# Routing of a mixture-of-experts layer: the last token tile's normed rows by ScalarE and GpSimd, and half a projection product ahead of the counts

## What is computed

```python
n2 = rms_norm(h, g_ffn[i]).reshape(b * s, d)
h = h + hier_moe(n2, w_group[i], b_group[i], w_router[i], b_router[i], w1[i], w3[i], w2[i]).reshape(b, s, d)
gate = jax.nn.sigmoid(rms_norm(h, g_ple[i]) @ w_ple_gate[i] + b_ple_gate[i])
h = h + gate * (p[i] @ w_ple_proj[i])

def hier_moe(xn, ...):                   # top 2 of 8 experts within the best of 4 groups
    gl = xn @ w_group + b_group
    grp = argmax(gl)
    el = (xn @ w_router + b_router), the 8 columns of grp
    top_l, top_i = lax.top_k(el, 2)
    counts = jnp.bincount(eid, length=32)
    # each expert's tokens are gathered into rows; per block of rows xb of expert e:
    hdn = jax.nn.silu(xb @ w1[e]) * (xb @ w3[e])
    ys = hdn @ w2[e]                     # weighted and added back to its tokens
```

## Time and profile before

| | us |
|---|---|
| median of 3 runs | 1689.8 |
| lowest and highest | 1689.41, 1690.76 |
| the profiled execution | 1689.12 |
| its span, first to last instruction | 1687.2 |

### The profile page before, as it was taken

One profiled execution on the slowest core, in us unless ns is written; L12 is line 12 of the kernel. 1 busy time (PEld: TensorE's weight loads), 2 busy tenths in 40 slices (PEclk: granted clock), 3 DMA queues, 4 the chain that ended last, 5 costly groups with the idle time before them and its releaser, 6 DMA issues.

```text
span 1687.2 us, 20190 instructions
## 1 busy us (share of the span) xinstructions
PE 1666.5 (99%) x7754; PEld 1007.6 (60%) x7754; DVE 882.4 (52%) x1509; ACT 386.7 (23%) x702; POOL 211.1 (13%) x279
## 2 busy tenths in 40 slices
PE   9999999999999999999999999999999999999999
PEld 5877888885433343434334455688855544667664
DVE  3755746765433232323225446666756654677663
ACT  3122212002100000000002212321245524544530
POOL 2334310001100000000001000010234420000000
PEclk9999999999999999999999999999999999999999
DMA  7312113254899999999996123114120021212101
GB/s 282 125 63 113 50 61 124 100 202 185 321 424 426 427 427 425 428 427 427 427 426 243 50 75 125 50 63 164 63 101 1 1 76 56 94 51 77 74 1 50
DMA packets 27715, 308.14 MB, mean 183 GB/s; under 512 B 4383, under 2 KB 4671, under 8 KB 10080
## 3 DMA queue, kind: packets, MB, share of 16 engines
q1 hardware_dynamic: 21168, 288.70, 42.1%
q0 software_dynamic: 6448, 18.10, 3.0%
HBM read 306.06 MB, written 4.19 MB: 184 GB/s over the span
## 4 chain that ended last, share of the span: by engine, by line
PE 92%; DVE 4%; DMA 2%; ACT 1%; issue 1%; POOL 0%; DVEq 0%; SPq 0%; ACTq 0%
PE ps L440 88%; PE ps L443 5%; DMA wring<-in_w 2%; DVE arena L1266 2%; ACT arena L2504 1%; DVE arena L1293 0%; DVE arena L1277 0%; DVE small L1281 0%; POOL small L2944 0%; ACT HT L2504 0%; DVE arena L1271 0%; DVE wring L1266 0%; DVE H L1266 0%; DVE arena L1350 0%; DVE ps L1266 0%
## 5 line engine op out<-in xcount | busy, mean ns | idle before, releaser
L440 PE MATMUL ps<-arena 128*64 128x512 f32 (+13 forms) x2484 | 533.8, 395 | 5.6 <-DMA wring<-in_w 1.7
L440 PEld LDWEIGHTS ps<-arena 128*64 128x64 f32 (+4 forms) x2484 | 249.1, 156 | 224.3 <-issue 213.0
L440 PE MATMUL ps<-wring,arena 128*64 128x512 f32 (+2 forms) x1048 | 345.1, 564 | 0.0
L1266 DVE TENSOR_TENSOR arena<-ps,arena 128x512 f32<-128x512 f32 (+1 forms) x196 | 134.1, 684 | 383.4 <-PE ps L440 230.5
L440 PE MATMUL ps<-wring,HT 128*128 128x512 f32 (+1 forms) x880 | 311.0, 505 | 4.8 <-ACT HT L2504 3.3
L440 PEld LDWEIGHTS ps<-wring,HT 128*128 128x128 f32 x880 | 163.5, 190 | 125.5 <-issue 112.7
L440 PE MATMUL ps<-HT,wring 128*128 128x512 f32 (+2 forms) x656 | 222.1, 501 | 0.0
L2504 ACT ACTIVATE arena<-ps 128x512 f32<-128x512 f32 (+4 forms) x155 | 82.7, 533 | 595.3 <-PE ps L443 305.5
L440 PE MATMUL ps<-wring 128*128 128x256 f32 x864 | 195.7, 380 | 0.0
L440 PEld LDWEIGHTS ps<-wring,arena 128*64 128x64 f32 (+1 forms) x1048 | 131.3, 151 | 87.4 <-issue 82.6
L1266 DVE TENSOR_TENSOR H<-ps,H 128x512 f32<-128x512 f32 x182 | 125.9, 691 | 97.6 <-PE ps L440 96.0
(11 more groups left out here) (125 smaller groups left out, 1007.8 us busy)
## 6 DMA issues: line engine op xcount, KB each, us to landing
wring<-in_w SPq DMA_DIRECT2D x48, 2048.0 KB, 22.8
wring<-in_dense SPq DMA_DIRECT2D x38, 2048.0 KB, 8.2
arena<-in_w SPq DMA_DIRECT2D x36, 2048.0 KB, 21.4
HT<-in_w SPq DMA_DIRECT2D x12, 2048.0 KB, 19.5
arena<-in_rows POOLq DMA_DIRECT2D x29, 256.0 KB, 4.0
wring<-in_dense SPq DMA_DIRECT2D x2, 1024.0 KB, 5.6
H<-in_x SPq DMA_DIRECT2D x4, 512.0 KB, 6.8
arena<-in_relb POOLq DMA_DIRECT2D x8, 256.0 KB, 8.6
```

What stands on the lines that cost most here:

```text
L440: return nc.tensor.matmul(o, l, r, start=start, stop=stop, skip_group_check=True)
L1266: done(nc.vector.tensor_tensor(o, a, b, op), tell)
```

## The change

The last tile's normed rows are no longer VectorE's. ScalarE writes `H[:, 3, :]` times the reciprocal root into `nbB[3]` (one instruction of 128x1024, with the columns reordered) right after its last copy of transposed rows. GpSimd waits for it and multiplies each half by its half of the gain row in place (two instructions of 128x512, signal `last_rows`), waits for them, and stores the rows. TensorE waits for `last_rows` instead of `nb` ahead of a = 3. The readers of the gain rows are now these two GpSimd instructions, so that slot 7's first load waits for them. The first half (k = 0) of `projection(0, 1)` stands ahead of `count`, with its wait for its weights, and the second half where the whole product was.

```diff
@@ TensorE, end of stage_a and stage_b
                 pe.wait_ge(S("wpp0"), 16)
                 for i in range(3):
                     projection(i, 0)
+                pe.wait_ge(S("wpp1"), 16)
+                projection(0, 1, (0,))
...
                 ins.then_inc(f.full, 1)
-                pe.wait_ge(S("wpp1"), 16)
-                projection(0, 1)
+                projection(0, 1, (1,))
...
                 for a in range(4):
-                    pe.wait_ge(S("nb"), saw("nb"))
+                    if a < 3:
+                        pe.wait_ge(S("nb"), saw("nb"))
+                    else:
+                        pe.wait_ge(S("last_rows"), 2)
@@ VectorE, normed_rows and stage_b
                     stt(o, x, small[:, 4 + i:5 + i], w, MUL, MUL, "nb" if h else "v")
-                    if i == 3:
-                        row_done(g[h])
...
                     stt(first[:, a, :], iota[:, 0:128], p8[:, 4 + a:5 + a], first[:, a, :], ALU.is_equal, ADD, "first")
-                normed_rows(3, g_ffn)
+                for h in range(2):
+                    rowed[g_ffn[h][0]] = S("last_rows"), h + 1
                 heard("gx")
@@ ScalarE, end of stage_a
                     for j in ((), (0,), (1, 2), (3,))[i]:
                         turned("B", j)
+                a.wait_ge(S("inv"), 10)
+                act(nbB[3].rearrange("t (k p) -> t k p", k=8), H[:, 3, :].rearrange("t (p k) -> t k p", k=8), ACT.Identity, "rt",
+                    scale=small[:, 7:8])
                 for i in range(3):
                     projected(i, 0)
@@ GpSimd
                 norm_root(i)
-                g.wait_ge(S("nb"), 5 + i)
+                if i < 3:
+                    g.wait_ge(S("nb"), 5 + i)
+                else:
+                    g.wait_ge(S("rt"), saw("rt"))
+                    for h, r in enumerate(ROWSEQ_B[2:]):
+                        o = nbB[3].rearrange("t (k p) -> t k p", k=8)[:, :, 64 * h:64 * h + 64]
+                        nc.gpsimd.tensor_tensor(o, o, rowbuf[r % NR].rearrange("t (p k) -> t k p", k=8), MUL
+                                                ).then_inc(S("last_rows"), 1)
+                    g.wait_ge(S("last_rows"), 2)
                 g.dma_start(n2d[i * 128:i * 128 + 128, :], nbB[i]).then_inc(S(f"keep{i % 2}"), 16)
```

## The result

| | before | after |
|---|---|---|
| median of 18 runs, us | 1690.27 | 1692.68 |
| lowest and highest | 1689.21, 1691.32 | 1690.60, 1694.61 |
| profiled execution, its span | 1689.12, 1687.2 | 1692.38, 1690.5 |

The ratio after to before is 1.0015 (95% interval 1.0008 to 1.0021): the change makes the kernel slower by 2.5 us, and the forecast was 0.7 faster. The range, 1687.7 to 1690.7, misses it by 2 us. The difference is less than 0.2% of the time, but the interval lies wholly above 1.

What follows compares the result with a forecast made beforehand. The weight-load stream, started by the end of w1, was taken as the bound, close to TensorE's queue. The half product's -0.86 plus 0.15 for contention made -0.7, so 1689.8 becomes 1689.1 us; range 1687.7 to 1690.7.

Steps and rivals of the forecast that it cites:

- What bounds the kernel: Expert loop: TensorE's queue and the weight-load stream are close bounds; the stream starts at w1's end, which must move.
- Rival (A): Expert loop: the load stream is not the bound, so TensorE's 1.3 us counts: 1688.5; chance 0.15.
- (C): Between `count` and w1: nothing moves, held by something unseen or delays eating the 0.86: 1689.8; chance 0.13.
- (D): GpSimd's reordered passes so slow that a = 3 waits; at 10 us each, 2.9 lost: 1692.7; chance 0.04.
- The half product: TensorE ahead of `count`: half the product fits the idle time, so everything to w1's end comes 0.86 us earlier.
- Off VectorE: VectorE between `first` and `tw`: 2.45 us of last-tile work leaves, so `rows` loses its wait and moves 1.43 earlier.
- ScalarE's instruction: ScalarE after its last copy: 1.06 us, perhaps twice that when reordered, ending between 410.5 and 411.6, hidden either way.
- What VectorE pays beside GpSimd: VectorE's chain to `cc`: slowed by GpSimd's passes by 0.15 us, between 0 and 0.45.
- Rival (B): VectorE's chain: GpSimd's two-input passes slow it by 1.35 us, more than the half product gives: 1690.3; chance 0.15.

Runs made afterwards that it cites:

- the last version: Changed kernel with GpSimd multiplying the last tile's residual by the gain first, then ScalarE scaling the product in place: median 1688.88 us, ratio 0.9994.
- the one-input experiment: Changed kernel with GpSimd's two passes multiplying by 1.0 instead of the gain row, last tile's gain left out: median 1689.74 us, ratio 0.9999.

## Why the prediction was wrong

**What bounds the kernel** held. The end of w1 starts the stream of loads, and the stream sets the end of the experts. The half product alone leaves `rows` where it was and still gains its 0.8 at slot 4's load; the last version moves `rows` 1.3 us earlier and gains no more than that. The DMA link is in the chain of both, with 1.25 and 1.87 us of waiting. Rival (A) is out. So is (C), since the half product alone moved the end of w1 by 0.8, and (D), since GpSimd's passes were over at 414.5 and nothing waited at a = 3.

**The half product** was right: -0.86 forecast, -0.8 at slot 4's load, with the work hidden in the idle time. **Off VectorE** was right in its mechanism: in the changed kernel `rows` starts behind w1 without a wait.

**ScalarE's instruction** took 2.16 us, the upper end of what I gave (twice 1.06). I called it hidden either way, and on ScalarE's own queue it was. But it starts GpSimd: the passes ran from 411.5 and not from 410.6, and so the whole 3.0 us lay beside the chain. GpSimd's 1.5 us each were within the bounds.

**What VectorE pays beside GpSimd** is the step that failed. I took 0.15 us, from a long instruction that grew by 0.37 ns per element, and so counted the exposed elements. The cost is not one of elements: an instruction of 16 elements paid what was left of GpSimd's current instruction. Two of them cost 0.87 + 1.28 = 2.15. The row I took it from had one input on GpSimd's side, and the one-input experiment shows that this is another, smaller cost (0.43 us of late `count` in place of 2.13). The row for VectorE alone was not alone either: it lay within a small GpSimd instruction and lost nothing to it. A chain longer by more than 0.3 us was the sign of being wrong that the prediction gave; it was longer by 2.1. Rival (B) had the right place and sign and said that two inputs might be worse; its 1.35 us also counted elements, and its condition (GpSimd at work until about 417, so some 3 us for each pass) was wrong: 3 us for both were enough.

**The clock** was in no step, and this is the second term that was missing. I treated a late `count` as a shift. TensorE's idle time grew from 0.88 to 2.16 us, and behind it the granted clock fell to 1.2 GHz for 3.4 us and took 1.7 us more. Over all profiles: with 0 to 1.58 us of idle time ahead of `count` (before and six others) it never fell there, with 2.16 to 3.01 in four of five. The balance without the fall is 2.13 - 0.86 = +1.3, near the 1.4 between the lowest groups; with it +3.0, near the profile's 3.3. The median of +2.4 lies between. In how many runs of the changed kernel the fall was behind `count` and in how many in the second block can't be told without their profiles; if the second block has it in half of the runs, as before, an estimate is 8 of 18 behind `count`. Whether idle time makes it likely, and why it comes in some executions only, stays open: the matmuls that filled the gap took the fall away in two profiles of two, a small number, and the fall at 1079 us needed no such gap.

**The range** allowed 0.7 us for what medians of this kernel stray. That is no even noise either: the median depends on how many of the runs had a fall. Before alone it was 1690.27 in one set and 1690.82, 1689.67 and 1689.49 in the sets beside the experiments. So a difference of one microsecond is read from groups of the same number of falls, and from the trace.

## What to carry to other kernels

Before work goes to GpSimd, list what VectorE does during it: beside a long GpSimd pass with two inputs, a VectorE instruction with two SBUF inputs may cost the whole rest of that pass, however short it is itself. Put such passes where VectorE is idle or reduces. Making them short alone helps little: in four pieces each, `count` was still 1.55 us late instead of 2.13. A wait on TensorE's path can cost more than its length: here the clock fell behind four of five waits of 2.2 to 3.0 us. And look at the single runs, not only at their median, when a change is worth a microsecond.

## What the runs showed of the hardware that I had not expected

- VectorE instructions of 128x16 with two SBUF inputs took 1.04 and 1.45 us instead of 0.17 beside GpSimd's two-input passes and ended 0.03 to 0.04 us after a pass. Beside passes of 128x128 a one-input `TENSOR_SCALAR` was held too (0.44), a reduction was not (0.17). Beside GpSimd's `TENSOR_TENSOR` of 128x32, 5.46 us long, a VectorE instruction of 128x1024 with two SBUF inputs was not held (1.22 us).
- GpSimd's pass over 128x512 took 1.5 us with two inputs and 1.5 with one, and 2.3 when both operands were read out of order (from `H` and the gain rows). ScalarE took 2.16 us for 128x1024 read out of order from `H` and 1.15 in order and in place.
- The clock's fall took 3.4 us at the lower level in each of the seven falls of the twelve profiles. The one at about 1079 us, in three of them, comes and goes from execution to execution of the same kernel: 1694.52 against 1692.38 and 1692.83 against 1690.63.
